# One split step without its wait, hidden layers opened chunk by chunk, and mask with extremum in one instruction

## What is computed

```
m = max(s);  p = exp(s - m);  o = (p @ v) / sum(p)        # both attentions, s masked with -inf
x = x + mixer(rmsnorm(x));  h = rmsnorm(x);  x = x + (silu(gate(h)) * val(h)) @ w_down
```

## Time and profile before

| | us |
|---|---|
| median of 3 runs | 1689.92 (1689.84 to 1690.18) |
| the profiled execution, its own time | 1691.72 |
| span of the profiled execution | 1689.9 |
| granted clock of TensorE, mean | 0.997 |

### The profile page before, as it was taken

One profiled execution on the slowest core, in us unless ns is written; L12 is line 12 of the kernel. 1 busy time (PEld: TensorE's weight loads), 2 busy tenths in 40 slices (PEclk: granted clock), 3 DMA queues, 4 the chain that ended last, 5 costly groups with the idle time before them and its releaser, 6 DMA issues. The chain is left out here.

```text
span 1689.9 us, 28488 instructions
## 1 busy us (share of the span) xinstructions
PE 1665.1 (99%) x10944; PEld 1497.1 (89%) x10944; DVE 1353.9 (80%) x2174; ACT 1086.8 (64%) x1832; POOL 754.0 (45%) x454
## 2 busy tenths in 40 slices
PE   9999999999999999999999999999999999999997
PEld 8998889998888899999788988889999878888887
DVE  7978887494987878895996699778887699579795
ACT  7676576675775584776654676657467665378572
POOL 8631115962110367764554521048675465351113
PEclk9999999999999999999999999999999999999999
DMA  8545655541555555453345456556455335546552
GB/s 305 165 155 191 209 171 179 199 124 50 190 187 191 190 172 188 161 184 125 127 161 189 147 176 212 168 181 199 152 175 175 125 125 174 175 138 200 192 182 87
DMA packets 81239, 287.10 MB, mean 170 GB/s; under 512 B 9168, under 2 KB 9680, under 8 KB 80976
## 3 DMA queue, kind: packets, MB, share of 16 engines
q1 hardware_dynamic: 79776, 282.10, 50.4%
q10 hardware_dynamic: 1328, 3.18, 0.5%
HBM read 283.90 MB, written 1.05 MB: 169 GB/s over the span
## 5 line engine op out<-in xcount | busy, mean ns | idle before, releaser
L553 POOL TENSOR_TENSOR w_lo<-w_raw,w_hi 128x1024 fp32r<-128x1024 f32 (+2 forms) x239 | 570.2, 2405 | 308.7 <-ACT w_hi L1500 225.3
L1500 ACT ACTIVATE w_hi<-w_raw 128x1024 fp32r<-128x1024 f32 (+1 forms) x544 | 543.1, 1033 | 253.8 <-PE lin L786 162.7
L553 DVE TENSOR_TENSOR w_lo<-w_raw,w_hi 128x1024 fp32r<-128x1024 f32 (+1 forms) x305 | 456.7, 1502 | 31.0 <-ACT w_hi L1500 30.0
L784 PE MATMUL lin<-hid_pair,w_hi 128*128 128x256 f32 x1152 | 329.9, 286 | 1.8 <-POOL w_lo L553 1.7
L785 PE MATMUL lin<-hid_pair,w_hi 128*128 128x256 f32 x1152 | 326.1, 283 | 0.0
L786 PE MATMUL lin<-hid_pair,w_lo 128*128 128x256 f32 x1152 | 326.1, 283 | 0.0
L784 PEld LDWEIGHTS lin<-hid_pair,w_hi 128*128 128x128 f32 x1152 | 221.1, 192 | 6.3 <-issue 5.5
L785 PEld LDWEIGHTS lin<-hid_pair,w_hi 128*128 128x128 f32 x1152 | 221.2, 192 | 0.2
L786 PEld LDWEIGHTS lin<-hid_pair,w_lo 128*128 128x128 f32 x1152 | 221.2, 192 | 0.0
L562 POOL TENSOR_TENSOR hid_pair<-arena,hid_pair 128x256 fp32r<-128x256 f32 x64 | 53.3, 839 | 326.2 <-ACT std L1575 178.3
L805 PE MATMUL logit<-h_pair,w_hi 128*128 128x512 f32 x540 | 146.7, 392 | 0.0
(11 more groups left out here) (407 smaller groups left out, 3581.6 us busy)
## 6 DMA issues: line engine op xcount, KB each, us to landing
w_raw<-in_upA SPq DMA_DIRECT2D x112, 512.0 KB, 4.5
w_raw<-in_upB SPq DMA_DIRECT2D x64, 512.0 KB, 4.6
w_raw<-in_xbc SPq DMA_DIRECT2D x48, 512.0 KB, 4.3
w_raw<-in_dnA SPq DMA_DIRECT2D x32, 512.0 KB, 4.5
w_raw<-in_dnB SPq DMA_DIRECT2D x32, 512.0 KB, 4.1
w_raw<-in_z SPq DMA_DIRECT2D x32, 512.0 KB, 4.4
w_raw<-in_gates SPq DMA_DIRECT2D x32, 512.0 KB, 4.4
w_raw<-in_ps SPq DMA_DIRECT2D x32, 512.0 KB, 4.0
```

Source lines behind the costliest of these rows:

```text
L553: eng.tensor_tensor(w_lo[slab.slot][:, half, part], w_raw[slab.slot][:, half, part], w_hi[slab.slot][:, half, part].bitcast(F32), ALU.subt ...
L784: nc.tensor.matmul(out, lhs[0], rhs[0], start=first, stop=False)
L1500: nc.scalar.activation(w_hi[slab.slot][:, half, part], w_raw[slab.slot][:, half, part], ACT.Copy)\
```

## The change

POOL no longer waits at j = 3 of a border. PE's first slab on normalised values in the hybrid layers waits for each rounded chunk by itself. In both attentions scaling, mask and extremum are one instruction, `tensor_tensor_reduce`: it writes (logit + mask) times a negative scale and keeps the minimum, which is the negated maximum; the exponential then has the scale -1. The semaphores `at_max` and `da_max` go, and ACT waits for `at_masked` and `da_masked`. In the dilated attention one maximum instruction of each of eight units goes, in the hybrid attention one of each of 2 x 4 units, and there the four heads' minima are written one by one.

```diff
--- before.py
+++ after.py
@@ -293,7 +293,6 @@
         s.qk_chain = sem("qk_chain")
         s.at_logits = sem("at_logits")
         s.at_masked = sem("at_masked")
-        s.at_max = sem("at_max")
         s.at_exp = sem("at_exp")
         s.at_p = sem("at_p")
         s.at_tr = sem("at_tr")
@@ -317,7 +316,6 @@
         s.ix_chain = sem("ix_chain")
         s.da_logits = sem("da_logits")
         s.da_masked = sem("da_masked")
-        s.da_max = sem("da_max")
         s.da_exp = sem("da_exp")
         s.da_chain = sem("da_chain")
         s.da_p = sem("da_p")
@@ -647,8 +645,6 @@
 
                 for k in range(COUNT[stage]):
                     j = k - (COUNT[stage] - 4)
-                    if j == 3 and n < 8:
-                        pool.wait_ge(s.h_lo_v, DC // 2 * n + 4)
                     split_lo(pool, slab_at(stage, k, l).ahead(SPLIT_AHEAD), 0)
                     if j in (0, 1) and n < 8:
                         norm_lo(n, (2 * j, 2 * j + 1))
@@ -1024,8 +1020,7 @@
                         wait_hi, wait_lo = scaled_number(UP_OPENING[layer])
 
                         def wait_chunk(c):
-                            if c == 0:
-                                wait_hi(KC - 1)
+                            wait_hi(c)
                             wait_lo(c)
                         slab_products_two(slab, k, wait_chunk)
                     else:
@@ -1792,8 +1787,8 @@
                     weights_hi(slab.ahead(ROUND_AHEAD))
             def at_exp(u):
                 n = DIL_G * (u % 2 + 1) * P
-                act.wait_ge(s.at_max, u + 1)
-                nc.scalar.activation(score[:, u % 2, 0:n], score[:, u % 2, 0:n], ACT.Exp,
+                act.wait_ge(s.at_masked, u + 1)
+                nc.scalar.activation(score[:, u % 2, 0:n], score[:, u % 2, 0:n], ACT.Exp, scale=-1.0,
                                      bias=small[:, 16 + u:17 + u], accum_out=small[:, 24 + u:25 + u]).then_inc(s.at_exp, 1)
 
             def at_copy(u):
@@ -1877,9 +1872,9 @@
 
                 def da_exp(u):
                     n = (u // 2 + 1) * P
-                    act.wait_ge(s.da_max, 4 * l + u + 1)
+                    act.wait_ge(s.da_masked, 4 * l + u + 1)
                     for i in range(QPK):
-                        ins = nc.scalar.activation(da_score[u % 2][:, i, 0:n], da_score[u % 2][:, i, 0:n], ACT.Exp,
+                        ins = nc.scalar.activation(da_score[u % 2][:, i, 0:n], da_score[u % 2][:, i, 0:n], ACT.Exp, scale=-1.0,
                                                    bias=small[:, 16 + i:17 + i], accum_out=small[:, 24 + i:25 + i])
                     ins.then_inc(s.da_exp, 1)
 
@@ -2358,12 +2353,10 @@
                 if u >= 2:
                     dve.wait_ge(s.at_tr, u - 1)
                 sc3 = score[:, u % 2, 0:DIL_G * n].rearrange("p (g k) -> p g k", g=DIL_G)
-                stt(sc3, logit[:, 0:DIL_G, 0:n], DIL_D ** -0.5,
-                    dil[:, DIL_AT[t]:DIL_AT[t] + DIL_G * n].rearrange("p (g k) -> p g k", g=DIL_G), ALU.mult, ALU.add)\
-                    .then_inc(s.at_masked, 1)
-                dve.wait_ge(s.at_masked, u + 1)
-                nc.vector.tensor_reduce(small[:, 16 + u:17 + u], score[:, u % 2, 0:DIL_G * n], AX_X, ALU.max, negate=True)\
-                    .then_inc(s.at_max, 1)
+                nc.vector.tensor_tensor_reduce(
+                    sc3, logit[:, 0:DIL_G, 0:n],
+                    dil[:, DIL_AT[t]:DIL_AT[t] + DIL_G * n].rearrange("p (g k) -> p g k", g=DIL_G),
+                    -DIL_D ** -0.5, -TAKEN, ALU.add, ALU.min, small[:, 16 + u:17 + u]).then_inc(s.at_masked, 1)
 
             ac = lc = mixer
 
@@ -2549,10 +2542,9 @@
                         dve.wait_ge(s.da_tr, 4 * l + u - 1)
                     sc4 = da_score[u % 2][:, :, 0:n]
                     for i in range(QPK):
-                        ins = stt(sc4[:, i, :], logit[:, i, 0:n], HD ** -0.5, sel[:, t, 0:n], ALU.mult, ALU.add)
+                        ins = nc.vector.tensor_tensor_reduce(sc4[:, i, :], logit[:, i, 0:n], sel[:, t, 0:n], -HD ** -0.5,
+                                                             -TAKEN, ALU.add, ALU.min, small[:, 16 + i:17 + i])
                     ins.then_inc(s.da_masked, 1)
-                    dve.wait_ge(s.da_masked, 4 * l + u + 1)
-                    nc.vector.tensor_reduce(small[:, 16:20], sc4, AX_X, ALU.max, negate=True).then_inc(s.da_max, 1)
 
                 dc = Chain(dve, s.da_chain, 4 * l)
 
```

## The result

The changed kernel takes 1682.16 us (median of 4 executions, 1682.11 to 1683.11); the kernel before took 1690.05 beside it (median of 4). The ratio is 0.995, with a 95% interval from 0.9933 to 0.9968: it is faster by half a per cent, clear of noise. Its profiled execution took 1682.21 us, 9.51 less than the profiled execution before.

A forecast was written before the change was run, and what follows sets the result against it. PE was taken as the bound, busy 1665.1 of 1689.9 us, so only its idle time and low clock could yield. Borders 5.07, attention 0.6 and clock 2.92 sum to 8.6: 1689.92 - 8.6 = 1681.3 us, range 1680.0 to 1688.0.

The forecast's parts named there:

- Borders: At seven borders, dropping POOL's wait starts its split about 3.9 us earlier and shortens PE's waits: 5.07 us.
- direct stop: PE's waits for POOL's `w_lo` go: 0.61 us at border 2, 0.60 at 4 and 6, 0.17 at 5 and 7.
- the second part of borders 5 and 7: Openings of the hybrid layers: POOL's remainders come 1.5 us earlier; whole border 1.33 us, bounds 0.17 and 1.9.
- Chunk-by-chunk wait: Hybrid-layer openings: PE's first matmul starts earlier, the fourth still follows POOL's pace: 0, bounds 0 and 0.83 us twice.
- Hybrid attention: Fused mask and extremum in both hybrid layers shorten DVE's work, but no PE wait ends on a mask: 0.
- Attention: Dilated attention: one 0.96 us fused instruction per pair lets PE start unit 3's logits 0.6 us earlier, bounds 0 to 0.65.
- what is late next: Dilated attention: with ACT's value-slab copy earlier, mask 2 ends near 380.17 and PE starts near 380.3, not 380.89.
- The clock: After the dilated attention's idle time, cut from 1.41 to about 0.8 us, PE's clock stays up: 2.92 us.
- I take the same offset for the changed kernel: Whole kernel: the profiled execution's 1.8 us above the median was carried over, turning 1683.1 into 1681.3 us.
- The first: Rival in the dilated attention: clock falls as before, only 5.07 + 0.6 us return; 1684.2 us, chance 0.27.
- The second: Rival: hybrid-layer openings give their gain back and the clock falls; 1686.9 us, chance 0.19 including nothing at the borders.
- The third: Rival: POOL's earlier split holds up DVE's remainders of chunks 6 and 7 at seven borders; 1696 us, chance 0.06.

The follow-up runs named there:

- e_undil: Changed kernel with the old mask and maximum put back in the dilated attention alone; profiled execution 1682.62 us, 2 of 6 executions higher.
- c_chunk: Kernel before with only the chunk-by-chunk wait for rounded chunks at the openings of the two hybrid layers; 1690.20 us.
- b_dilated: Kernel before with mask and extremum fused in the dilated attention alone; median 1688.20 us over eleven executions.
- j_shift: Changed kernel with unit 0's logit matmuls done three times, 1.3 us more PE work before the idle time; lowest level 1683.8 us, 5 of 7 executions above.
- i_reorder: Changed kernel with the dilated attention's start reordered: PE's unit 0 transposes and unit 2 logits inside the last value slab, some DVE work earlier; 1681.38 us.
- k_reorder_shift: Changed kernel with the dilated attention's start reordered, plus 1.3 us more PE work ahead of it; 1682.54 us.
- after_again: Changed kernel, unchanged, run again in more executions; its profiled execution took 1683.28 us.

## Why the prediction was right, and where it was not

The time was forecast at 1681.3 and came out at 1682.16. Two errors of opposite sign nearly cancel, the borders' gain taken 0.9 too small and the start of the sum 1.8 too low; that the total fits so well is luck. Against the profiled execution the sum was 8.6 us and 9.5 came. Against the median it was the same 8.6 and 7.9 came.

**Borders: 5.07 forecast, 5.97 measured with the wait alone.** The mechanism held at each step: the split starts right behind `h_lo_v` at 4n+2 and ends 0.49 us ahead of the remainders (0.47 forecast), DVE's split takes 1.21 us, and POOL's four remainders come 1.5 us earlier against the border. What was mis-sized is the price of a direct stop. I took the printed idle time, 0.61, 0.60, 0.60 and twice 0.17, together 2.15; the same five stops were worth 0.84, 0.84, 0.83, 0.40 and 0.39, together 3.30. Border 2's second wait was undervalued in the same way, 0.61 against 0.30. Elsewhere I was a little too generous: border 4 gave back 0.09 and border 6 brought 0.07 where I expected 0.15 each, and the second part of borders 5 and 7 brought 1.09 and 1.08 (1.16 each). Of PE's four later waits there, 0.53 and 0.69 in each hybrid layer are left.

**Chunk-by-chunk wait: 0 forecast, 0 measured.** **Hybrid attention: 0 forecast, 0 measured**; DVE's saving of 0.86 us for each unit lies within the 0.24 to 1.0 that the forecast's durations leave. The extremum is an instruction of its own, as the prediction quoted it, but at 0.083 us each the saving is not "next to nothing".

**Attention: 0.6 forecast, 0.4 to 0.6 measured.** The fused instruction is one pass, 0.96, with 0.08 for the extremum (0.09 taken), and mask 2 is what PE waits for, as forecast. The first wait lost 0.7 us. The step that failed is "what is late next": I followed the chain to unit 3's logits and stopped there. Beyond the borders' 1.26 us, ACT's copy and rounding, and with them POOL's split, came 1.2 us earlier, but DVE's remainder only 0.6, as mask 2 ahead of it waits for PE. So POOL now starts first, by 0.05 us, the remainder takes 2.85 us (1.23 alone), and PE's next slab product waits for it. In the kernel before DVE was first, and POOL's split bore the delay, for which PE did not wait. That the sum came near all the same owes something to luck.

**The clock: 2.92 forecast; 1.7 of the median, and not for the reason given.** The price was right for the profiled execution: the levels of 1691.7 and 1688.6 differ by 3.1, and instruction by instruction PE gains 3.5 us in the attention between the two profiled executions, 0.55 of it by the fused instruction, as e_undil's trace has it. But the profiled execution was one of the dearer ones; the median execution lies 1.7 above the lowest level, and 11 of 57 lie on it. The step that failed is "I take the same offset for the changed kernel". The profiled execution lay 1.8 us above the median because its clock was low for longer (c_chunk's profiled execution, at 1690.06 with the same idle time, loses 1.6 us less behind it), and I had already taken that whole loss out. Without the fall profile and median agree (1682.21 and 1682.16), so the forecast should have been 1691.72 - 8.6 = 1683.1; the borders' 0.9 more make it 1682.2. By the lowest levels before and after differ by 1688.6 - 1682.2 = 6.4 us, and 1.7 more is the clock, by the reading of the levels.

That the shorter idle time is what holds the clock is not shown as a rule. b_dilated speaks for it, 0 of 11 against 46 of 57, though POOL and DVE change places behind the idle time there too; e_undil and j_shift speak against it. What is shown is that without any idle time there the five executions each of i_reorder and k_reorder_shift lie within 0.9 and 0.5 us. What decides with idle time there stays open, and so does how much of the changed kernel's 7 in 9 is owed to its present place.

**The rivals.** The first (the clock falls as before, 1684.2) came true in two of nine executions by their level, at 1683.1 and 1683.3, the second of them with a trace: there it costs only some 1 us, partly since PE, being slower, no longer has the wait of 0.36. The second did not happen: the openings kept their gain. The third was right in kind, and for a single border nearly in size: up to 2.0 us forecast, 0.6 to 1.8 measured where the engines do meet. But the forecast added its price, 7 us at halfway, to the kernel before and came to 1696. Counted from there, the lowest levels give 4.3 us; it is 10.7 only from the changed kernel. The measured time is 1694.0.

## What to carry over

Look at single executions before summing against a profile: where they lie at levels, ask at which level the profiled one is, and do not carry its offset from the median along. Price a stop of PE by the distance of starts against an undisturbed stretch, and over some matmuls behind it, not by the printed idle time. When a wait goes, follow the other engines past the point where PE is released: where two engines exclude each other, a few tenths of a microsecond can change which of them starts first, and so which of them is late. Moving other products into the hole (i_reorder) took both waits at once.

## What was not expected of the hardware

The granted clock fell in some executions of one kernel and not in others, behind the same idle time: by the levels in 46 of 57 before and 2 of 9 after. The cost came in steps, 1688.6, 1690.2, 1691.7 and 1693.4 us in the kernel before. The Trainium skill (TensorE: Matmul & The Clock Gate, "Part 1: The HAM clock gate") has PE's activity watched on a beat that runs freely and does not begin anew with a kernel; levels that vary from one execution to the next, with all else the same, would fit that, but no run here shows the beat. An idle time of 1.41 us was passed at full clock in e_undil's profiled execution (1682.62 us), and one of 0.75 us was not in after_again's. That POOL's split and DVE's subtraction exclude each other was expected; its price was not: two remainders of 0.83 us took 2.65 when POOL had started 0.37 us ahead of them, and one of 1.23 us took 2.85 when POOL was ahead by 0.05. With DVE ahead by 0.58 it was POOL that took 2.31 where it takes 1.81.
